# Chunk scores of an HGRN2 head, spread over the contraction steps of a projection tile

## What is computed

```
b = cumsum(log_f)                      # decay within the chunk
q_dec = q * exp(b)
scores = where(causal, q_dec @ (k * exp(-b)).T, 0)
o = scores @ v + q_dec @ state
state = exp(b_last) * state + (k * exp(b_last - b)).T @ v
o = o * rsqrt(mean(o * o) + eps)       # per head, then norm_g, silu(gate), w_out
```

## Time and profile before

| | |
|---|---|
| runs, median | 1723.18 us |
| runs, lowest and highest | 1716.9 and 1723.3 us |
| profiled execution, span | 1719.9 us |
| PE busy | 1696.3 us, 99% |
| DVE busy, ACT busy | 798.4 us, 46%; 642.7 us, 37% |
| mean granted PE clock | 0.982 |

### The profile page before, as it was taken

One profiled execution on the slowest core, in us unless ns is written; L12 is line 12 of the kernel. 1 busy time (PEld: TensorE's weight loads), 2 busy tenths in 40 slices (PEclk: granted clock), 3 DMA queues, 4 the chain that ended last, 5 costly groups with the idle time before them and its releaser, 6 DMA issues.

```text
span 1719.9 us, 22142 instructions
## 1 busy us (share of the span) xinstructions
PE 1696.3 (99%) x8249; PEld 1446.8 (84%) x8249; DVE 798.4 (46%) x1363; ACT 642.7 (37%) x1088; POOL 20.8 (1%) x40
## 2 busy tenths in 40 slices
PE   7999999999999999999999999999999999999997
PEld 6888888888888689888899888889888889888886
DVE  6564574556465632444433344442344442334445
ACT  4443354343344333343332333333233333233333
POOL 0000000000000000000000000000000000000000
PEclk9999999998998999999999999999999999999999
DMA  6522321321321124433314323332333333333321
GB/s 208 158 69 73 92 64 45 110 73 61 91 69 61 39 85 117 98 81 84 89 54 122 98 62 87 91 86 91 113 93 80 93 68 98 98 93 82 87 54 62
DMA packets 247998, 149.47 MB, mean 87 GB/s; under 512 B 47040, under 2 KB 227648, under 8 KB 247920
## 3 DMA queue, kind: packets, MB, share of 16 engines
q1 hardware_dynamic: 203328, 139.69, 29.4%
q0 software_dynamic: 2608, 8.39, 1.5%
q10 hardware_dynamic: 41984, 0.27, 1.3%
HBM read 146.02 MB, written 6.50 MB: 89 GB/s over the span
## 4 chain that ended last, share of the span: by engine, by line
PE 97%; DVE 1%; ACT 1%; issue 0%; DMA 0%; SPq 0%; DVEq 0%; ACTq 0%
PE proj L422 80%; PE inner L565 4%; PE inner L686 3%; PE inner L654 2%; PE inner L422 2%; PE inner L674 2%; PE inner L642 1%; PE inner L587 1%; PE inner L590 1%; PE inner L576 1%; PE inner L569 0%; DMA v<-x 0%; DVE v L1405 0%; PE inner L544 0%; PE inner L531 0%
## 5 line engine op out<-in xcount | busy, mean ns | idle before, releaser
L1023 DVE TENSOR_TENSOR w_lo<-raw,w_hi 128x1024 fp32r<-128x1024 f32 x252 | 308.0, 1223 | 483.2 <-ACT w_hi L735 482.1
L422 PE MATMUL proj<-u_hi,w_hi 128*128 128x512 f32 x1280 | 514.6, 402 | 0.0
L422 PE MATMUL proj<-u_hi,w_lo 128*128 128x512 f32 x1280 | 503.1, 393 | 0.0
L422 PE MATMUL proj<-u_lo,w_hi 128*128 128x512 f32 x1280 | 503.0, 393 | 0.0
L735 ACT ACTIVATE w_hi<-raw 128x1024 fp32r<-128x1024 f32 x252 | 265.3, 1053 | 133.6 <-PE proj L422 118.5
L422 PEld LDWEIGHTS proj<-u_hi,w_lo 128*128 128x128 f32 x1280 | 243.1, 190 | 52.7
L422 PEld LDWEIGHTS proj<-u_lo,w_hi 128*128 128x128 f32 x1280 | 243.7, 190 | 48.7
L422 PEld LDWEIGHTS proj<-u_hi,w_hi 128*128 128x128 f32 x1280 | 243.4, 190 | 48.8 <-issue 0.3
L422 PE MATMUL proj<-w_hi,u_hi 128*128 128x512 f32 x472 | 191.8, 406 | 6.7 <-issue 3.7
L422 PE MATMUL proj<-w_lo,u_hi 128*128 128x512 f32 x472 | 189.2, 401 | 0.0
L422 PE MATMUL proj<-w_hi,u_lo 128*128 128x512 f32 x472 | 188.9, 400 | 0.0
(11 more groups left out here) (156 smaller groups left out, 1497.0 us busy)
## 6 DMA issues: line engine op xcount, KB each, us to landing
raw<-at_w_in SPq DMA_DIRECT2D x160, 512.0 KB, 4.1
raw<-hg_w_in SPq DMA_DIRECT2D x64, 512.0 KB, 4.2
raw<-hg_w_out SPq DMA_DIRECT2D x16, 512.0 KB, 3.6
raw<-at_w_out SPq DMA_DIRECT2D x16, 512.0 KB, 4.4
v<-x SPq DMA_DIRECT2D x4, 512.0 KB, 6.5
bias_tiles<-ext_rows POOLq DMA_DIRECT2D x1, 2048.0 KB, 11.8
bias_tiles<-ext_rows POOLq DMA_DIRECT2D x2, 1024.0 KB, 17.6
bias_n<-bias_tiles POOLq DMA_DIRECT2D x16, 128.0 KB, 4.1
```

What stands on the lines that cost most here:

```text
L422: ins = nc.tensor.matmul(bank[:, :], stationary(a), moving(b), start=(first and n == 0), stop=(last and n == 2))
L1023: nc.vector.tensor_tensor(w["lo"][:, slot, :], raw[:, slot, :], w["hi"][:, slot, :].bitcast(F32), ALU.subtract).then_inc(w_ready, 1)
```

## The change

The scores of heads 0 to 2 of each quad no longer come behind the first half of the next head's F tile. They are cut in four blocks (one for each block of 128 tokens, four score matmuls each) and one block is issued behind each of the four contraction steps of the second half. The transposes of the keys follow behind that half, and updates, outputs and norm sum each come one half later than before. `proj_done` is still raised with the tile's last big matmul, ahead of the fourth block. The wait for `keys_ready` stands ahead of the first block. The scores of a quad's last head are one run behind the first half of what follows, as before. The same instructions are issued, in another order.

```diff
-            def head_tile(layer, q, n, half):
+            def head_tile(layer, q, n, half, between=None):
...
-                if half:
-                    ins.then_inc(proj_done, 1)
+                    if half and k == KT - 1:
+                        ins.then_inc(proj_done, 1)
+                    if between is not None:
+                        between(k - half * KT // 2)
...
             def scores(g):
 
-                pe.wait_ge(keys_ready, g + 1)
                 for b in range(ST):
-                    for j in range(NC):
-
-                        seen = (j + 1) * CH
-                        ins = nc.tensor.matmul(p_sc[0:seen, b * P + j * CH:b * P + (j + 1) * CH], keys[:, b, j, 0:seen],
-                                               qd[:, b * P + j * CH:b * P + (j + 1) * CH], start=True, stop=True)
-                ins.then_inc(scores_done, 1)
+                    score_block(g, b)
+                transpose_keys(g)
+
+            def score_block(g, b):
+
+                if b == 0:
+                    pe.wait_ge(keys_ready, g + 1)
+                for j in range(NC):
+
+                    seen = (j + 1) * CH
+                    ins = nc.tensor.matmul(p_sc[0:seen, b * P + j * CH:b * P + (j + 1) * CH], keys[:, b, j, 0:seen],
+                                           qd[:, b * P + j * CH:b * P + (j + 1) * CH], start=True, stop=True)
+                if b == ST - 1:
+                    ins.then_inc(scores_done, 1)
+
+            def transpose_keys(g):
+
                 for b in range(ST - 1):
                     ins = nc.tensor.transpose(p_kT[:, b * P:(b + 1) * P], keys[:, b, NC, :], ident[:, :])
                 ins.then_inc(kT_done, 1)
...
                     for half in range(2 * HG.per_head):
-                        head_tile(HG, q, HG.per_head * h + half // 2, half % 2)
-                        if h:
-                            recurrence(head(q, h - 1), h - 1, half)
+                        spread = None
+                        if h and half == 1:
+                            spread = lambda b: score_block(head(q, h - 1), b)
+                        head_tile(HG, q, HG.per_head * h + half // 2, half % 2, spread)
+                        if h and half == 1:
+                            transpose_keys(head(q, h - 1))
+                        elif h and half > 1:
+                            recurrence(head(q, h - 1), h - 1, half - 1)
```

## The result

The changed kernel takes 1744.83 us (median of four executions, 1737.08 to 1753.89) against 1723.24 us before: a ratio of 1.0136, 95% interval 1.0083 to 1.0189. It is slower, as forecast, and inside the stated range of 1720 to 1746 us, but by 21.6 us where 10.8 were forecast from the median. Its executions differ by 17 us, those of before by 12. The profiled one is the fastest, 1737.08 us, with a span of 1735.2; so 1.9 us lie around the span.

A forecast was written before the change was run, and what follows sets the result against it. TensorE (PE), busy for 99% of the span, was taken as the bound. Clock gain, seams, waits and lost clock summed as -14.0 + 6.2 + 16.9 + 1.5 + 1.5 = +12.1 us, giving 1734 us, range 1720 to 1746.

The forecast's parts named there:

- part 3: PE waits for keys behind the moved norm sum: eight at heads, three at value tiles, one in last quad; 16.9 us.
- The signs named for this part: PE waits on VectorE's keys at about 12 places, 17 us; head stretch about 24.9 us at clock 1.00.
- part 2: Three more seam pairs between short and big matmuls at each of twelve heads: 6.2 us added on PE.
- part 1: Spreading the scores of heads 0 to 2 of each quad removes the clock falls behind their bursts: 14.0 us gained.
- part 4: Clock lost to the new waits: 1.5 us at the eight waiting heads, 1.5 us more at last heads' bursts.
- The whole clock term: Clock gain at spread heads less clock lost to new waits there and at quads' ends: -14.0 + 1.5 + 1.5 us.
- The third: Rival: clock still falls in spread halves, half or all of 14.0 us stays, 1741 to 1748 us; chance 0.17.
- Its sign: PE's clock shows more than three falls outside the bursts of the quads' last heads.
- The first rival: Keys come in time ahead of the first block, no wait: 1715.4 us, 1709 if seams are free; chance 0.13.

The follow-up runs named there:

- shift: Changed kernel's later recurrence kept, but scores in one run behind the whole second half; 1733.21 us, ratio 1.0058 to the kernel before.
- first_half: Kernel before with score blocks behind the four steps of F's first half, recurrence at its old places; 1720.76 us, ratio 0.9980 to before.
- keysfirst: Changed kernel with keys made independent of the norm sum, except the last quad's last head; 1709.39 us, ratio 0.9923 to before.
- mid: Kernel before with score blocks behind the first half's last two and second half's first two steps, recurrence unmoved; 1704.46 us, ratio 0.9895.
- early: Kernel before with score blocks behind the first half's last three and second half's first step, recurrence unmoved; 1710.50 us, ratio 0.9922.
- mid_tails: As mid, plus last-head scores of the first three quads spread over the first value tile; 1706.02 us, ratio 0.9889 to the kernel before.
- lump: Changed kernel with all four score blocks in one run at the first block's place; 1748.96 us, ratio 1.0146 to the kernel before.
- its repeat: Changed kernel timed again with no edit, giving the second profile; 1750.09 us, ratio 1.0146 to the kernel before.

## Why the prediction was right in its sign and wrong in its size

- **The waits (part 3) came as worked out.** The forecast priced distances between starts, so I take those. PE's timeline at a head, at a quad's end and at the end of the last quad:

```profile
87.13 0.39 PE L422 MATMUL proj<-u_hi,w_lo 128*128 128x512 f32 x1
...
140.17 0.39 PE L422 MATMUL proj<-w_hi,u_lo 128*128 128x512 f32 x1
142.28 0.22 PE L573 MATMUL inner<-rows,keys 128*32 128x32 f32 x1 [1.72 <-DVE keys L1194]
...
567.38 0.39 PE L609 MATMUL inner<-osq_lo,ones_r 128*128 128x512 f32 x1
...
572.66 0.50 PE L422 MATMUL proj<-y_hi,w_hi 128*128 128x512 f32 x1 [0.76 <-DVE y_lo L1215]
...
575.45 6.01 PE L573 MATMUL inner<-rows,keys 128*32 128x32 f32 x32 [1.82 <-DVE keys L1194]
```

  Less the 0.32 us of an entry without a wait, a head waits for 1.1 us (87.13 to 88.56; 1.0 in the last quad) as forecast, and three quads' ends for 1.8 (140.17 to 142.28), as forecast. In the last quad the norm sum and the scores are 8.07 us apart, as they were (8.06), with twelve big matmuls fewer between them: all 2.7 us show. They are split in two waits, 0.76 us ahead of the last three big matmuls, which need the last y, and 1.82 ahead of the scores; I had not named the first. Sum: 16.6 us against 16.9. (As idle time it is 15.0 us on the keys and 0.9 on y, 15.5 above before.) `shift` shows the ends alone (7.0 us), `first_half` the heads alone (8.3), `keysfirst` shows that it is the place behind the norm sum that makes them. The signs named for this part came too: twelve places, a stretch of 24.63 us at a clock of 1.00, 0.32 us into a block.
- **The seams (part 2) were too dear.** Forecast 6.2 us (12 x 3 x 0.175 is 6.3), measured 3.2. The distance into a block is 0.32 us as read (89.93 to 90.25), but a block of eight then takes 0.82 us (88.56 to 89.38) where eight of the burst take (233.20 - 229.62) / 4 = 0.90, up to the first transpose of before:

```profile
233.20 0.53 PE L569 MATMUL inner<-ident,keys 128*128 128x128 f32 x3
```

  I had priced the edges and kept the inside.
- **The gain (part 1) is real and was not got.** 14.0 us of falls at the heads were to go. Without a wait, or with one of 0.3 us, they go entirely: none at twelve heads in the profiles of `mid`, `keysfirst`, `early` and `mid_tails`.
- **The step that failed is part 4**, the clock that the new waits cost. I took one short fall at 1.5 us for the eight waiting heads, and 1.5 us more at the quads' ends. Two things were mis-sized. A fall in a spread half lasts 10.2 us and costs 4.5, most likely since blocks and seams go on behind it (in `lump`, with the same waits and no block behind the burst, none is longer than 6.8); I priced it from bursts, behind which only big matmuls come. And there were two and three of them in the two profiles, 9.0 and 13.5 us. At the ends the falls grew as well: from 3.4 and 6.8 us to 10 us at the last one in the first profile and at all four in the second. Such a fall costs 71.78 - (68.98 - 1.55) = 4.4 us there, by the stretches from a quad's end to the next quad's first block in the first profile (a fall of 3.4 us) and in the second (one of 10.2 us):

```profile
142.28:211.26 68.98, 68.98 (x325) 57.34 (x325) 35.15 (x53) 24.01 (x32) 0.00 (x0) 0.98 0.30 85
```

```profile
136.31:208.09 71.78, 71.78 (x325) 59.65 (x325) 35.25 (x53) 24.01 (x32) 0.00 (x0) 0.93 0.29 82
```

  The whole clock term was to be -11.0 us (-14.0 + 1.5 + 1.5). In the first profile it was -14.0 + 9.0 + 1.2 = -3.8 (the ends cost 3 x 1.55 + 4.4 = 9.0 for 7.8 before), in the second -14.0 + 13.5 + 9.6 = +9.1 (4 x 4.35 = 17.4 at the ends).
- **The sums close.** First profile: 16.6 + 3.2 - 3.8 = 16.0, measured 1735.2 - 1719.9 = 15.3. Second: 16.6 + 3.2 + 9.1 = 28.9, less 1.5 us by which its first block comes sooner (62.47 for 63.93; a fall near 17 us, which every profile has, is 3.4 us long there and 6.8 in the other two): 27.4, measured 26.8.
- **The rivals.** The third, to which I gave 0.17, is what happened. It has clock falling in the spread halves through blocks, waits and transposes together, half or all of the 14.0 us lost again, and 1741 to 1748 us; the spread heads lost 9.0 and 13.5 us, and the median is 1744.8. That it fits the time so well is in part luck: it has neither the growth of the falls at the quads' ends nor the 3 us that the seams came cheaper. Its sign, more than three falls outside the last heads' bursts, did not come, since it counts falls and not their length. Of its three ingredients the wait is the one that has to be there: in the profiles of the change, its repeat and `first_half`, 6 of 24 heads with a wait of about 1.0 us have a fall, and in those and the others none of 55 spread heads without a wait. The first rival (keys in time) holds for `mid` and `keysfirst`: 1704.5 and 1709.4 for the 1715.4 that I worked out.

The Trainium skill, TensorE: Matmul & The Clock Gate, the table of its section on why this matters, asks for no idle gaps of over about 3 us. Here the clock fell at six of 24 places where PE was idle for about 1.0 us ahead of a block of short matmuls, and at none of eight with 0.24 to 0.36 us.

## What to carry to other kernels

Before you move a step later, look for what hangs on it two links on, through another engine's fixed order: here the norm sum held the keys of the next head only because the output product stood ahead of the decays on VectorE, and the norm ahead of the exponential on ScalarE. Issuing the blocks two steps earlier with the rest of the recurrence left in place, or another order on VectorE and ScalarE, turned a loss of 1.4 to 1.5% into a gain of 0.8 to 1.1%. Short matmuls cost more than their own time when they let the clock fall, and spreading them among big ones is a cure only if PE doesn't wait there for long: 1.0 us was too much here, 0.3 us was not. Price a wait on PE by its length and by the clock after it: 13 us of waits were worth 41.

## What the runs showed of the hardware

- A single wait of about 1.0 us ahead of a block of eight 32-column score instructions sometimes (6 of 24 heads) lowers TensorE's clock for 10.2 us, if more such blocks follow; the same blocks without a wait kept it at 1.00 at all 55 heads profiled. What decides which of the waiting heads fall stays open.
- The 10.2-us falls at quads' ends all begin before the burst's first score or within 0.5 us behind it (136.69 for a score at 136.31); the shorter ones at such ends begin 1.3 us behind it or later (145.29 for 142.28).
- Executions of the changed kernel differ by up to 17 us, in step with the mean clock (0.974 to 0.984), and the kernel before, with one wait of 0.2 us on the keys, by 10 to 13 on a chip (0.977 to 0.985). The four kernels that spread the scores and have no waits at heads, or waits of 0.3 us, repeat within about 4 us.
- The short weight load of the first score is not begun under the big matmul ahead (0.32 us into a block in place of 0.23), but a block of eight runs faster than eight in a long burst, 0.82 against 0.90 us.
